# The second boundary of a hybrid block kernel: an early sum of the shift's share from a second copy of two weight units, another order of splits, and two units in turns

## The reference

```python
x = x + g2[:, None, :] * (y @ w_out[l])
h = rmsnorm(x, norm_ffn2_g[l]) * (1.0 + sc3[:, None, :]) + sh3[:, None, :]
x = x + 0.5 * g3[:, None, :] * ((silu(h @ w1) * (h @ w3)) @ w2)
```

## Time and profile before

| | us |
|---|---|
| median of 3 runs | 1014.27 (1013.31 to 1015.56) |
| the profiled execution | 1013.98 |
| its span | 1012.2 |

### The profile page before, as it was taken

The page is one execution under the profiler, slowest core; times in us unless marked ns, Lnnn a source line. Parts: engine busy times, 40 slices in busy tenths (PEclk is TensorE's granted clock), DMA queues, the critical chain, the costliest instruction groups (busy, mean ns, idle before and its releaser), DMA issues.

```text
span 1012.2 us, 13155 instructions
## 1 busy us (share of the span) xinstructions
PE 987.6 (98%) x4524; PEld 808.7 (80%) x4524; DVE 550.3 (54%) x772; ACT 349.3 (35%) x542; POOL 51.9 (5%) x79
## 2 busy tenths in 40 slices
PE   7999999999999999999999998899999999999997
PEld 3678888888888888788888886788888888888886
DVE  3767876787675445743475437844344344333332
ACT  4243232232342223622165534533223223323221
POOL 2011111011000000000000320000000000000000
PEclk9999999999999999999999999999999999999998
DMA  9757866686453333223220112233333323333332
GB/s 327 242 165 251 264 196 207 205 268 207 143 178 94 96 96 101 71 84 104 76 76 21 43 63 63 65 110 94 104 89 97 104 85 101 98 95 96 95 94 84
DMA packets 178989, 127.88 MB, mean 126 GB/s; under 512 B 5408, under 2 KB 165986, under 8 KB 178960
## 3 DMA queue, kind: packets, MB, share of 16 engines
q1 hardware_dynamic: 170560, 97.93, 32.3%
q0 software_dynamic: 8400, 29.58, 8.8%
HBM read 125.39 MB, written 2.10 MB: 126 GB/s over the span
## 4 chain that ended last, share of the span: by engine, by line
PE 52%; DVE 4%; ACT 1%; issue 1%; DVEq 0%; ACTq 0%
PE pb L853 49%; PE pb L890 1%; DVE wl L1389 1%; DVE sacc L1400 1%; PE pb L872 0%; DVE hl L1421 0%; DVE ubuf L1428 0%; DVE acc L1521 0%; DVE gl L1508 0%; DVE xres L1502 0%; DVE ptl L1897 0%; PE pb L1178 0%; PE pb L1370 0%; DVE nmax L1878 0%; PE pb L1229 0%
## 5 line engine op out<-in xcount | busy, mean ns | idle before, releaser
L853 PE MATMUL pb<-hh,wh 128*128 128x512 f32 x880 | 346.0, 393 | 4.8 <-DVE wl L1389 2.4
L853 PE MATMUL pb<-hh,wl 128*128 128x512 f32 x880 | 342.7, 389 | 0.0
L853 PE MATMUL pb<-hl,wh 128*128 128x512 f32 x880 | 342.5, 389 | 0.0
L1389 DVE TENSOR_TENSOR wl<-raw,wh 128x1024 fp32r<-128x1024 f32 x156 | 191.0, 1224 | 242.7 <-ACT wh L429 242.5
L429 ACT ACTIVATE wh<-raw 128x1024 fp32r<-128x1024 f32 x159 | 168.3, 1059 | 447.5 <-PE pb L853 433.9
L853 PEld LDWEIGHTS pb<-hh,wh 128*128 128x128 f32 x880 | 165.2, 188 | 42.5 <-DVE wl L1389 4.3
L853 PEld LDWEIGHTS pb<-hh,wl 128*128 128x128 f32 x880 | 165.2, 188 | 34.6
L853 PEld LDWEIGHTS pb<-hl,wh 128*128 128x128 f32 x880 | 165.3, 188 | 33.2
L853 PE MATMUL pb<-gh,wh 128*128 128x512 f32 x368 | 144.0, 391 | 0.9 <-issue 0.9
L853 PE MATMUL pb<-gh,wl 128*128 128x512 f32 x368 | 143.7, 390 | 0.0
L853 PE MATMUL pb<-gl,wh 128*128 128x512 f32 x368 | 143.7, 390 | 0.0
(11 more groups left out here) (261 smaller groups left out, 718.6 us busy)
## 6 DMA issues: line engine op xcount, KB each, us to landing
raw<-in_ffn_w_dram SPq DMA_DIRECT2D x102, 512.0 KB, 3.8
ada_ring<-in_ada_w_dram POOLq DMA_DIRECT2D x56, 512.0 KB, 5.3
raw<-in_ffn_w_dram SPq DMA_DIRECT2D x32, 448.0 KB, 3.4
raw<-in_w_in_dram SPq DMA_DIRECT2D x17, 512.0 KB, 3.7
ada_start<-in_ada_w_dram SPq DMA_DIRECT2D x16, 512.0 KB, 9.2
raw<-in_w_out_dram SPq DMA_DIRECT2D x8, 512.0 KB, 3.4
x_nat<-in_x_dram SPq DMA_DIRECT2D x4, 512.0 KB, 5.2
out_dram<-o_nat SPq DMA_DIRECT2D x8, 256.0 KB, 2.9
```

The source lines that it names most:

```text
L853: last = pe.matmul(o, a, b, start=start and j == 0 and t == 0, stop=stop and j == len(pairs) - 1 and t == 2)
L1389: dve.tensor_tensor(wl[par][:, :], raw[par][:, :], wh[par][:, :].bitcast(F32), ALU.subtract).then_inc(lo_ready, 1)
```

## The change

- SP loads a second copy of U_A2 and U_A2 + 1 (512 KB each) into a new place, `raw_late`, which lies over buffers that the heads no longer use; the issue stands behind the load of output unit 1 and waits for the last head unit.
- `late_share` replaces the two calls of `share`: the same 16 instructions, the two units in turns, reading `raw_late`, at o = 3 on DVE ahead of the split of output unit 5. Each waits for the last but one.
- At each o of 3 to 6 DVE's split of unit o + 2 stands ahead of the updates (at o = 7 where it was), and the plain parts and rests of an upper unit's tiles come one turn later, by the table PLAIN_AT.
- Tile 1's two units of the second FFN go through `first_pair`, and DVE's split of the second of them stands after the seventh tile's first instruction instead of after all tiles.
- In the input projection the sum of the kv norm stands in the middle of unit 4 instead of after unit 3.

```diff
--- before.py
+++ after.py
@@ -199,6 +199,7 @@
         (xg,), _ = place(hh_at, ("xg", [P, DT, SEQ], F32))
         (o_nat,), _ = place(hl_at, ("o_nat", [P, TT, D_MODEL], F32))
 
+        (raw_late,), _ = place(region + 8 * 4 * SEQ, ("raw_late", [P, 2, UW], F32))
         late_h, late_l = gh[:, FT - DT:FT, :], gl[:, FT - DT:FT, :]
         group_wide = (sq[:, 0, :], sq[:, 1, :], turned[:, 0:SEQ], turned[:, SEQ:2 * SEQ])
 
@@ -239,6 +240,7 @@
         plain_hi, plain_lo, plain_used = sem("plain_hi"), sem("plain_lo"), sem("plain_used")
         share_step, share_done, share_copied, zm_ready = sem("share_step"), sem("share_done"), sem("share_copied"), sem("zm_ready")
         zkv_raw = sem("zkv_raw")
+        late_landed = [sem("late_landed0"), sem("late_landed1")]
         first_raw, first_normed = sem("first_raw"), sem("first_normed")
         zkv_copied, zq_copied = sem("zkv_copied"), sem("zq_copied")
         kr_roped, kr_dup, krh_ready, krl_ready = sem("kr_roped"), sem("kr_dup"), sem("krh_ready"), sem("krl_ready")
@@ -279,6 +281,7 @@
         O_BANK = (0, 1, 2, 3, 4, 5, 0, 1)
 
         O_UNITS = ((0, 0), (0, 1), (0, 2), (1, 0), (1, 1), (1, 2), (0, 3), (1, 3))
+        PLAIN_AT = {3: (), 4: (0, 1), 5: (2, 3), 6: (4, 5), 7: (6, 7)}
         P_OFF = [P * i * (i + 1) // 2 for i in range(TT + 1)]
 
 
@@ -359,6 +362,10 @@
                              wukvv[:, :, h, 0:QK_NOPE]).then_inc(kn_landed[h % 2], 16)
             for o, (upper, pair) in enumerate(O_UNITS):
                 load(U_O + o, o % 2, woutv[:, 4 * upper:4 * upper + 4, 2 * P * pair:2 * P * (pair + 1)])
+                if o == 1:
+                    sp.wait_ge(unit_done, U_O)
+                    for b, v in enumerate((w1v, w3v)):
+                        sp.dma_start(raw_late[:, b, :].rearrange("p (k f) -> p k f", k=DT), v[1][:, :, 0:P]).then_inc(late_landed[b], 16)
             with sp.Fori(0, FT) as i:
                 up_units(U_A2, 1, i)
             down_units(U_B2, 1)
@@ -787,8 +794,8 @@
                     for d in (2 * pair, 2 * pair + 1):
                         act.wait_ge(x_upd, DT + d + 1)
                         square(N_FFN2, d, (SQ_BASE[N_FFN2] + d) % 2, xres[:, d, :])
-                    for d in (2 * pair, 2 * pair + 1):
-                        plain_part(late_h, d, 2)
+                for d in PLAIN_AT[o]:
+                    plain_part(late_h, d, 2)
             root(N_FFN2, D_MODEL)
             for k in range(DT):
                 norm_hi(AP_BASE[N_FFN2] + k, hh[:, k, :], mods[:, 6 * DT + k:6 * DT + k + 1])
@@ -859,7 +866,11 @@
 
             def h_product(o, b, hbase):
 
-                for k in range(DT):
+                return h_steps(o, b, hbase, range(DT))
+
+            def h_steps(o, b, hbase, ks):
+
+                for k in ks:
                     pe.wait_ge(hl_ready, hbase + k + 1)
                     last = three(o, [(cols(wh[b], k), cols(wl[b], k), hh[:, k, :], hl[:, k, :])], k == 0, k == DT - 1)
                 return last
@@ -1111,12 +1122,14 @@
                 z_step(1, k)
             for j in range(2, KT + QT + 1):
                 unit(U_Z + j)
-                h_product(pb[j][:, :], j % 2, AP_BASE[N_MIX]).then_inc(unit_done, 1)
-                if j == KT + 1:
+                if j == KT + 2:
+                    h_steps(pb[j][:, :], j % 2, AP_BASE[N_MIX], range(HALF))
                     pe.wait_ge(sq_added, ADD_BASE[N_KV] + KT)
                     norm_sum(N_KV, sacc, AP_BASE[N_KV])
-                if j == KT + 2:
+                    h_steps(pb[j][:, :], j % 2, AP_BASE[N_MIX], range(HALF, DT)).then_inc(unit_done, 1)
                     norm_spread(N_KV)
+                else:
+                    h_product(pb[j][:, :], j % 2, AP_BASE[N_MIX]).then_inc(unit_done, 1)
             pe.wait_ge(sq_added, ADD_BASE[N_Q] + QT)
             norm_sum(N_Q, sacc, AP_BASE[N_Q])
 
@@ -1355,9 +1368,7 @@
             for k in range(HALF, DT):
                 a_step(1, k)
             pe.wait_ge(x_upd, 2 * DT)
-            for b in range(2):
-                unit(U_A2 + 2 + b)
-                h_product(pb[b][:, :], b, AP_BASE[N_FFN2]).then_inc(unit_done, 1)
+            first_pair(U_A2 + 2, AP_BASE[N_FFN2])
             with pe.Fori(2, FT) as i:
                 up_tile(U_A2, 1, i, N_FFN2)
             down(U_B2, 1, N_FINAL, 0, DT // 2)
@@ -1507,6 +1518,19 @@
                 dve.wait_ge(plain_hi, hi_base + d + 1)
                 dve.scalar_tensor_tensor(out=lo_t[:, d, :], in0=xres[:, d, :], scalar=a_cols[:, which, d:d + 1],
                                          in1=hi_t[:, d, :].bitcast(F32), op0=ALU.mult, op1=ALU.subtract).then_inc(plain_lo, 1)
+
+            def late_share(shift_mod):
+
+                for k in range(DT):
+                    for b in range(2):
+                        part, col = acc[:, b * P:(b + 1) * P], mods[:, shift_mod * DT + k:shift_mod * DT + k + 1]
+                        src = raw_late[:, b, k * P:(k + 1) * P]
+                        if k == 0:
+                            dve.wait_ge(late_landed[b], 16)
+                            dve.tensor_scalar(part, src, col, None, ALU.mult).then_inc(share_step, 1)
+                        else:
+                            dve.wait_ge(share_step, 16 + 2 * k + b - 1)
+                            dve.scalar_tensor_tensor(out=part, in0=src, scalar=col, in1=part, op0=ALU.mult, op1=ALU.add).then_inc(share_step, 1)
 
             def share(n, b, shift_mod, turn_):
 
@@ -1956,30 +1980,24 @@
             for o in range(3, len(O_UNITS)):
                 upper, pair = O_UNITS[o]
 
+                last = o == len(O_UNITS) - 1
                 if o == 3:
+                    late_share(6)
+                if not last:
                     unit_lo(U_O + o + 2)
                 if upper:
                     for d in (2 * pair, 2 * pair + 1):
                         update(d, O_BANK[d], mods[:, 5 * DT + d:5 * DT + d + 1], U_O + o + 1, DT)
-                if o == len(O_UNITS) - 2:
-                    share(U_A2, 0, 6, 1)
-                if o != 3 and o != len(O_UNITS) - 1:
-                    unit_lo(U_O + o + 2)
-                if o == len(O_UNITS) - 2:
-                    share(U_A2 + 1, 1, 6, 1)
-                if upper:
                     for d in (2 * pair, 2 * pair + 1):
                         if d < DT - 1:
                             add_square(N_FFN2, d, (SQ_BASE[N_FFN2] + d) % 2)
-                if o == len(O_UNITS) - 1:
+                if last:
                     unit_lo(U_O + o + 2)
-                if upper:
-                    for d in (2 * pair, 2 * pair + 1):
-                        plain_rest(d, 2, late_h, late_l, DT)
+                for d in PLAIN_AT[o]:
+                    plain_rest(d, 2, late_h, late_l, DT)
             inverse(N_FFN2)
             share_copy(1)
-            apply_model(N_FFN2, 2, 6, among={4: lambda: split_lo(U_A2 + 2, 0)})
-            split_lo(U_A2 + 3, 1)
+            apply_model(N_FFN2, 2, 6, among={4: lambda: split_lo(U_A2 + 2, 0), 6: lambda: split_lo(U_A2 + 3, 1)})
             for b in range(2):
                 dve.wait_ge(first_raw, b + 1)
                 part = turned[:, b * SEQ:(b + 1) * SEQ]
```

## The result

The changed kernel takes 1006.66 us (median of 4 runs, 1005.95 to 1007.64) against 1013.79 for the kernel before (4 runs, 1011.83 to 1015.56): ratio 0.9931, 95% interval 0.9910 to 0.9952, so 7.1 us less, between 5 and 9. The forecast was 5.8 less, with a range that began at 1006.8.

A forecast was written before the change was run, and what follows sets the result against it. PE, 98% busy, was taken as the bound, so only its waits or low clock could give time. -0.82 - 6.15 + 1.15 = -5.8 us: 1008.2 us profiled, 1008.5 median, range 1006.8 to 1011.2.

The forecast's parts named there:

- from the last head to the spread: Second boundary: spread moves from 641.94 to 635.8, by two split waits, the sums' wait and the clock: -6.15 us.
- tile 1's pair: Second FFN's two units in turns: a wait inside the pair and a later tile 2, +1.15 us.
- Part 1: Input projection: kv norm's sum in the middle of a unit no longer waits for its square, -0.82 us.
- Part 2: Second copy and early share: load wait costs nothing, share covered by VectorE's 6.99 us idle; cost 0.
- Part 3: Output projection, splits ahead of plain parts: 1.10 + 1.13 + 2.2 at the sums + 1.7 of clock, -6.15 us.
- Part 4: Tile 1's units in turns: late second split and late Sigmoid start tile 2 1.15 us later; +1.15 us.
- the paragraph of the sum: Whole kernel: terms add to -5.8 us, taken from one profiled execution of 1013.98 us, giving 1008.2.
- (a): Rival: clock still falls, at the pair's waits or the sums; one fall costs 1.7 us, 1010.2; chance 0.13.
- (d): Rival: clock falls at the pair's waits and stays low through it, 9.6 us, so 1018.1; chance 0.05.
- (b): Rival: splits stay late because ACT, not the share, sets them; 2.2 us of gain lost, 1010.7; chance 0.10.
- (c): Rival: tile 1's pair loses nothing by the turns, 1007.3 us; chance 0.08.
- (e): Rival: another wait ahead of the sums takes all of the gain, about 1014 us; chance 0.04.

The follow-up runs named there:

- LAG = 5: Changed kernel with the second unit of tile 1's pair five steps behind the first instead of three: 1006.34 us.
- products in the wait: Kernel before with nine products of constants (384 columns each) in PE's wait before the sums: 1012.18 us, ratio 0.9979.
- the order alone: Kernel before with only splits ahead and plain parts one turn later, shares in their old place: 1015.25 us, ratio 1.0023.
- the kv sum alone: Kernel before with only the kv norm's sum moved to the middle of unit 4: 1011.52 us, ratio 0.9982.
- the early share alone: Kernel before with only the second copy and the share instructions moved early, old order and no turns: 1007.48 us, ratio 0.9945.

## Why the prediction was right and where it was wrong

| step | forecast | marks |
|---|---|---|
| kv sum | -0.82 | -0.97 |
| from the last head to the spread | -6.15 | -6.13 |
| tile 1's pair | +1.15 | +1.08 |
| the end | 0 | +0.17 |
| start of the execution | none | -1.05 |
| sum | -5.82 | -6.90 |

The steps of the changed kernel came as laid out. Part 1 was right. Part 2 was right: the copies were issued at 552.08, 50.6 us before VectorE wanted them where the bound said 41, and the share was covered. Part 3: the order of work on VectorE and ACT came out as it was laid out by hand; the spread is 6.13 us nearer to the last head than in the trace of before. Of this the first sum came 4.54 us sooner (forecast 4.4) and the stretch from the second sum to the spread took 1.58 less (forecast 1.7). Part 4 was right in both its losses: the pair's wait (0.76 listed, with the restart the 1.0 forecast) and tile 2's (0.37 listed), and the reason is the lag, as LAG = 5 shows.

What failed is the base under these steps, in the paragraph of the sum. It took one execution of the kernel before, 1013.98 us, took off the 5.8, and carried everything ahead of the change over unchanged, with no term and no bound for the start. The start measured 1.05 us less in the traced pair (404.56 against 405.61), and that is most of what lies between the 1008.2 us forecast for the profiled execution and its 1006.94. The second execution of the changed kernel, which started at 405.81, took 1008.22. The start moved by 1.7 us between four executions of one kernel (404.19 to 405.91), so with four runs on each side it alone can carry the median past the end of the range, which it missed by 0.1 us; that the median lies outside and not just inside is chance.

A second term was mis-sized: the clock's in part 3. 1.7 us was read from one execution and taken for all. Against a kernel without the fall it measured 1.6 in two executions of the kernel before and 3.2 in the other two. This does not touch the time of the changed kernel, but it does touch the difference: with two long falls in four the mean gain would be 6.6 us, with four in six 6.9, an estimate from the marks, where the forecast had 5.8 from a trace with a short fall. The remeasured difference of 6.4 us (ratio 0.9937, 5.1 to 7.8 us) and the first, 7.1 (5 to 9), fit either and the forecast as well.

Of the rivals, (a) and (d) did not come: the clock is 1.00 through the sums and the pair, in both traces of the changed kernel. Against them stood the waits at 613 and 619, for which the row shows the clock from 615 to 620 only; from 610 to 615 and from 620 to 625 it is 1.00 as well. The Trainium skill, "TensorE: Matmul & The Clock Gate", Part 1, was cited at (a) with the rule that only activity lifts the low clock; waits of 0.71, 0.76 and 0.37 us within 13 us did not lower the clock here, so no run of the changed kernel shows that risk. The products in the wait add that idle time alone does not decide it: there the clock fell although PE had stood for only 0.41 us before the sums. (b) did not come either: the splits were in time, and in the order alone, where the shares stand as before, the wait for the split of tile 1's first unit grew from 0.87 to 1.44 us, so the share and not ACT held it. (c) did not come with three steps of lag; with five it does, 0.15 us below the pair of before. (e) did not come: no other wait took the gain.

What was not tried: to hold the clock at the start, between 20 and 30 us, and any other way to hold it through the sums in the kernel before.

## What to carry to other kernels

A reduction that no one needs for 40 us can stand in the middle of a chain of splits and look cheap; moved into idle time of its engine, at the price of a second load, it gave some five of the six us up to the spread, 1.6 of them by the clock. An order of splits is worth something only once nothing long stands between them: alone it lost 2.3 us. When two streams take turns, the lag has to be read from when the second one's operand is ready; three steps cost 1.1 us here, five gave 0.15. And a forecast that is laid from one execution inherits that execution's clock: here the same kernel differed by 1.7 us in one place and by 1.6 in another.

## What the runs showed of the hardware

The same kernel, same instructions, falls to the lower clock (1.2 GHz, a granted clock of 0.50) around the same sums in each of four executions, but for two different lengths: some 3.4 us at 0.50, which cost 1.6, or some 6.8 us, which cost 3.2, nothing between. The traces of the kv sum alone and the order alone add two long ones. Before each fall of these four PE had had a wait of 2.0 us; the fall then began about 0.4 us after the sums started in the earliest case and 1.8 in the latest. Nine products of 384 columns in that wait did not prevent it in the one trace of them. In the changed kernel the same one-column products, without the wait, left the clock at 1.00, and so they did with the early share alone. Between 20 and 30 us the clock was 1.00 in three executions of 14 and 0.83 to 0.85 in the others, about 1 us of time. And a group of eight small products took 0.1 us longer when PE had stood before it (0.91 against 0.81).
